# Two expert tiles added from on-chip memory, and gathered rows weighted on TensorE

## The reference

```python
w = jnp.take_along_axis(scores, idx, axis=-1)      # the two chosen experts of each token
w = w / jnp.sum(w, axis=-1, keepdims=True)
combine = jnp.sum(jax.nn.one_hot(idx, N_EXPERTS, dtype=F32) * w[..., None], axis=1)
gate = jnp.einsum('td,edf->tef', t, w_gate_l)
up = jnp.einsum('td,edf->tef', t, w_up_l)
act = jax.nn.silu(gate) * up * combine[..., None].astype(gate.dtype)
return jnp.einsum('tef,efd->td', act, w_down_l).reshape(B, N, D)
```

## Time and profile before

| what | us |
|---|---|
| three runs | 2059.05, 2059.27, 2053.49 (median 2059.05) |
| the profiled execution, its own time | 2056.28 |
| its span, first to last instruction | 2054.5 |
| TensorE busy | 1912.6 (93%) |
| VectorE busy | 1080.4 (53%) |
| ACT busy | 884.8 (43%) |
| GpSimd busy | 314.5 (15%) |
| mean granted TensorE clock | 0.976 of full |

### The profile page before, as it was taken

One profiled execution on the slowest core, in us unless ns is written; L12 is line 12 of the kernel. 1 busy time (PEld: TensorE's weight loads), 2 busy tenths in 40 slices (PEclk: granted clock), 3 DMA queues, 4 the chain that ended last, 5 costly groups with the idle time before them and its releaser, 6 DMA issues. The chain is left out here.

```text
span 2054.5 us, 31276 instructions
## 1 busy us (share of the span) xinstructions
PE 1912.6 (93%) x12731; PEld 1617.7 (79%) x12731; DVE 1080.4 (53%) x1766; ACT 884.8 (43%) x1423; POOL 314.5 (15%) x120
## 2 busy tenths in 40 slices
PE   6999999999999979999779998898999998899993
PEld 4899866699999857777578997677999987577762
DVE  4385367641433256777573734665243334577763
ACT  4443455532222235566454435555222233466653
POOL 1303100032224120000111121000212331000003
PEclk9999999999999999999979999999999999999996
DMA  7422477725612159999441220002222222999954
GB/s 262 131 62 64 147 247 256 240 88 199 211 62 73 47 212 361 315 309 318 156 167 44 75 72 13 1 1 92 89 67 72 73 68 114 376 422 369 311 189 174
DMA packets 163921, 336.34 MB, mean 164 GB/s; under 512 B 10434, under 2 KB 121666, under 8 KB 149316
## 3 DMA queue, kind: packets, MB, share of 16 engines
q1 hardware_dynamic: 151488, 299.63, 41.9%
q0 software_dynamic: 5760, 20.97, 2.7%
q10 hardware_dynamic: 6532, 13.74, 2.1%
HBM read 334.58 MB, written 53.74 MB: 189 GB/s over the span
## 5 line engine op out<-in xcount | busy, mean ns | idle before, releaser
L728 POOL TENSOR_TENSOR wlo<-raw,whi 128x2048 fp32r<-128x2048 f32 x46 | 216.1, 4697 | 1053.2 <-ACT whi L752 1053.2
L2007 DVE TENSOR_TENSOR xw_gu_lo<-xw_gu_raw,xw_gu_hi 128x2048 fp32r<-128x2048 f32 x96 | 218.9, 2284 | 53.7 <-ACT xw_gu_hi L1788 35.6
L171 PE MATMUL psum<-h_hi,whi 128*128 128x320 f32 (+2 forms) x896 | 215.3, 313 | 9.0 <-DVE h_lo L156 6.5
L171 PE MATMUL psum<-h_hi,wlo 128*128 128x320 f32 (+2 forms) x896 | 213.0, 310 | 0.0
L171 PE MATMUL psum<-h_lo,whi 128*128 128x320 f32 (+2 forms) x896 | 213.0, 310 | 0.0
L171 PE MATMUL psum<-whi,h_hi 128*128 128x256 f32 x720 | 210.2, 292 | 0.5 <-ACT v_tok L866 0.5
L171 PE MATMUL psum<-wlo,h_hi 128*128 128x256 f32 x720 | 203.6, 283 | 0.0
L171 PE MATMUL psum<-whi,h_lo 128*128 128x256 f32 x720 | 203.6, 283 | 0.0
L1788 ACT ACTIVATE xw_gu_hi<-xw_gu_raw 128x2048 fp32r<-128x2048 f32 x96 | 178.1, 1907 | 7.6 <-DMA xw_gu_raw<-w_e_up 7.6
L2159 PE MATMUL psum<-xw_d_raw,act_T 128*128 128x512 f32 x400 | 179.9, 592 | 0.9 <-ACT act_T L1818 0.9
L832 ACT ACTIVATE prob<-psum,small_stats 128x640 f32<-128x640 f32 (+1 forms) x160 | 112.0, 705 | 133.1 <-DVE small_stats L1194 133.0
(11 more groups left out here) (319 smaller groups left out, 3657.3 us busy)
## 6 DMA issues: line engine op xcount, KB each, us to landing
xw_d_raw<-w_e_down SPq DMA_DIRECT2D x50, 1024.0 KB, 9.0
xw_gu_raw<-w_e_gate SPq DMA_DIRECT2D x48, 1024.0 KB
xw_gu_raw<-w_e_up SPq DMA_DIRECT2D x48, 1024.0 KB
raw<-w_in SPq DMA_DIRECT2D x46, 1024.0 KB, 5.4
wm_rest<-w_mod SPq DMA_DIRECT2D x40, 1024.0 KB, 5.3
y_rows<-y_sel SPq DMA_DIRECT2D x50, 512.0 KB, 9.5
h_sel<-h_rows SPq DMA_DIRECT2D x48, 512.0 KB, 7.5
h_rows<-c_zero ACTq DMA_DIRECT2D x5, 2560.0 KB, 11.2
```

The source lines that it names most:

```text
L171: mm = pe.matmul(dst, st, mv[q], start=start and n == 0, stop=stop and n == 2)
L728: pool.tensor_tensor(wlo[i % 2][:, :, :], raw[i % 2][:, :, :], whi[i % 2][:, :, :].bitcast(F32), ALU.subtract).then_inc(w_lo, 1)
L2007: dve.tensor_tensor(gu_lo[i % 2][:, n, :, :], gu_raw[i % 2][:, n, :, :], gu_hi[i % 2][:, n, :, :].bitcast(F32), ALU.subtract).then_inc(x_l ...
```

## The change

The results of tiles 23 and 24 are no longer stored and gathered. They stay in the two y_sel buffers, and TensorE adds them by products with a matrix `kept_w` of 128 slots by 128 tokens, one for each of the two tiles and five token tiles, which holds the token's weight where the token sits in that slot and zero elsewhere. A token's row number in the kept tiles is turned into row `row_kept` for the gather; that row of y_rows is cleared once, early in layer 0, by a small DMA on ACT's queue. The gathers wait for the stores of tiles up to 22. The weighting by ACT and VectorE goes: the gathered rows are multiplied on TensorE by diagonal matrices `w_diag` which hold the weights. All 32 products of a token tile accumulate in one PSUM region, already turned. VectorE builds marks and diagonals at the stage's start, TensorE turns the marks, VectorE copies them out of PSUM. The gather buffers lie elsewhere, and the low parts of the next layer's weights stand behind the first residuals.

```diff
--- before.py
+++ after.py
@@ -512,7 +512,13 @@
 
-y_ab = [at(f"y_ab{t}", [P, 2, D], (20 + 8 * t) * K if t < 4 else Z + 104 * K) for t in range(TT)]
+y_ab = [at(f"y_ab{t}", [P, 2, D], off) for t, off in enumerate((28 * K, 40 * K, Z + 104 * K, Z + 80 * K, Z + 88 * K))]
+pos_g = at("rows_gathered", [P, 2, TT], Z + 141 * K + 256, I32)
+w_diag = at("combine_diag", [P, 2, TT, P], RT + 2560)
+kept_w = [at(f"kept_tile_w{h}", [P, TT, P], RT + 8000 * h) for h in range(2)]
+kept_mark = [at(f"kept_tile_marks{h}", [P, TT, P], Z + 32 * K + 2560 * h) for h in range(2)]
+kept_key, kept_f, kept_r, kept_v = (at(f"kept_{x}", [P, 2, n], RT + 10592 + off) for x, n, off in (
+    ("key", TT, 0), ("factor", TT, 64), ("rows", 2 * TT, 128), ("weights", 2 * TT, 224)))
 sq_e = [at(f"sq_e{i}", [P, KD, P], Z + (112 + 4 * i) * K) for i in range(2)]
...
@@ -589,10 +595,14 @@
     return (n if kind == "s" else NE + n) * P
+row_kept = row0(N_TILES - 2)
+assert row0(N_TILES - 1) == row_kept + P and row_kept + 2 * P == SLOTS and (N_TILES - 2) % 2 == 1
 LOGIT_STEPS = 4
 ROUTE_STEPS = 15
 ROW_STEPS = 28
 IDX_STEPS = 44
+GATHER_STEPS = 46
+KEPT_STEPS = 78
 
...
@@ -987,6 +997,8 @@
     branch_high(2)
+if first and n == 2:
+    act.dma_start(y_rows[row_kept:row_kept + 1, :], a["c_zero"][0:1, :]).then_inc(s_rows0, 16)
 if first and 2 <= n < 7:
...
@@ -1739,8 +1751,6 @@
     sp.dma_start(fin_bc[:, :], a["final_norm_g"].partition_broadcast(P)).then_inc(f_g, 16)
-store_y(N_TILES - 2)
-store_y(N_TILES - 1)
 if last:
...
@@ -1762,13 +1772,14 @@
             in_=h_tok[:, t, :], in_offset=None).then_inc(k_s, 16)
-pool.wait_ge(y_st[0], 16 * ((N_TILES + 1) // 2))
-pool.wait_ge(y_st[1], 16 * (N_TILES // 2))
+pool.wait_ge(r_st, GATHER_STEPS)
+pool.wait_ge(y_st[0], 16 * ((N_TILES - 1) // 2))
+pool.wait_ge(y_st[1], 16 * ((N_TILES - 2) // 2))
 for t in range(TT):
     for s in range(2):
         pool.indirect_dma_start(
-            out=y_ab[t][:, s, :], out_offset=None, in_=y_rows,
-            in_offset=bass.IndirectOffsetOnAxis(ap=pos_ab[:, s, t:t + 1], axis=0)).then_inc(y_ld[t], 16)
+            out=y_ab[t][:, s, :], out_offset=None, in_=y_rows[0:row_kept + 1, :],
+            in_offset=bass.IndirectOffsetOnAxis(ap=pos_g[:, s, t:t + 1], axis=0)).then_inc(y_ld[t], 16)
 if last:
...
@@ -1854,16 +1865,8 @@
         act.activation(whi[c][:, :, :], raw[c][:, :, :], ACT.Copy).then_inc(nx_hi, 1)
-def scale_a(t):
-    act.wait_ge(y_ld[t], 32)
-    act.activation(y_ab[t][:, 0, :], y_ab[t][:, 0, :], ACT.Copy, scale=w_ab[:, 0, t:t + 1]).then_inc(m_za, 1)
-
-scale_a(0)
 if not last:
-    scale_a(1)
     for t in range(TT - 1):
-        if t + 2 < TT:
-            scale_a(t + 2)
         if t >= 2:
...
@@ -1998,6 +1999,29 @@
 assert n_st[0] == IDX_STEPS
+rows_2t, w_2t = pos_f[:, 0:2 * TT], w_ab[:, :, :].rearrange("p s t -> p (s t)")
+step(dve.tensor_scalar(kept_r[:, 0, :], rows_2t, float(row_kept), None, ALU.min))
+step(dve.tensor_copy(pos_g[:, :, :].rearrange("p s t -> p (s t)"), kept_r[:, 0, :]))
+assert n_st[0] == GATHER_STEPS
+for h in range(2):
+    step(dve.scalar_tensor_tensor(out=kept_r[:, h, :], in0=rows_2t, scalar=row_kept + P * h - 0.5, in1=rows_2t,
+                                  op0=ALU.is_gt, op1=ALU.mult))
+    step(dve.scalar_tensor_tensor(out=kept_v[:, h, :], in0=rows_2t, scalar=row_kept + P * h - 0.5, in1=w_2t,
+                                  op0=ALU.is_gt, op1=ALU.mult))
+step(dve.tensor_tensor(kept_r[:, 0, :], kept_r[:, 0, :], kept_r[:, 1, :], ALU.subtract))
+step(dve.tensor_tensor(kept_v[:, 0, :], kept_v[:, 0, :], kept_v[:, 1, :], ALU.subtract))
+step(dve.tensor_tensor(kept_key[:, :, :], kept_r[:, :, 0:TT], kept_r[:, :, TT:2 * TT], ALU.add))
+step(dve.tensor_tensor(kept_f[:, :, :], kept_v[:, :, 0:TT], kept_v[:, :, TT:2 * TT], ALU.add))
+for h in range(2):
+    step(dve.tensor_scalar(kept_key[:, h, :], kept_key[:, h, :], -(row_kept + P * h - 1.0), None, ALU.add))
+for h in range(2):
+    for t in range(TT):
+        step(dve.tensor_scalar(kept_mark[h][:, t, :], iota_1[:, :], kept_key[:, h, t:t + 1], kept_f[:, h, t:t + 1],
+                               ALU.is_equal, ALU.mult))
+for s in range(2):
+    for t in range(TT):
+        step(dve.tensor_scalar(w_diag[:, s, t, :], ident[:, :], w_ab[:, s, t:t + 1], None, ALU.mult))
+assert n_st[0] == KEPT_STEPS - 2
 
...
@@ -2034,6 +2058,12 @@
 h_low(1)
+dve.wait_ge(k_t, KD + 1)
+for h in range(2):
+    dve.tensor_copy(kept_w[h][:, 0:4, :].rearrange("p t s -> p (t s)"), psum[:, 7 - 2 * h, :])
+step(dve.tensor_copy(kept_w[0][:, 4, :], psum[:, 6, 0:P]))
+step(dve.tensor_copy(kept_w[1][:, 4, :], psum[:, 6, P:2 * P]))
+assert n_st[0] == KEPT_STEPS
 lo(2, "g")
...
@@ -2049,17 +2079,13 @@
 
-if not last:
+def next_low(c):
     dve.wait_ge(x_gu, N_TILES)
-    for c in range(2):
-        dve.wait_ge(nx_hi, c + 1)
-        dve.tensor_tensor(wlo[c][:, :, :], raw[c][:, :, :], whi[c][:, :, :].bitcast(F32),
-                          ALU.subtract).then_inc(nx_lo, 1)
+    dve.wait_ge(nx_hi, c + 1)
+    dve.tensor_tensor(wlo[c][:, :, :], raw[c][:, :, :], whi[c][:, :, :].bitcast(F32),
+                      ALU.subtract).then_inc(nx_lo, 1)
+
 for t in range(TT + 4):
-    if t < TT:
-        dve.wait_ge(m_za, t + 1)
-        dve.scalar_tensor_tensor(out=y_ab[t][:, 0, :], in0=y_ab[t][:, 1, :], scalar=w_ab[:, 1, t:t + 1],
-                                 in1=y_ab[t][:, 0, :], op0=ALU.mult, op1=ALU.add).then_inc(m_zb, 1)
     if last and 3 <= t < TT + 3:
...
@@ -2071,6 +2097,8 @@
     ins.then_inc(x_step, 1)
+if not last and 1 <= t < 3:
+    next_low(t - 1)
 if last and 2 <= t < TT + 2:
...
@@ -2176,10 +2204,18 @@
 gate_up_first()
+pe.wait_ge(r_st, KEPT_STEPS - 2)
+for h in range(2):
+    for t in range(4):
+        pe.transpose(psum[:, 7 - 2 * h, t * P:(t + 1) * P], kept_mark[h][:, t, :], ident[:, :])
+for h in range(2):
+    mm = pe.transpose(psum[:, 6, h * P:(h + 1) * P], kept_mark[h][:, 4, :], ident[:, :])
+mm.then_inc(k_t, 1)
 turn_h(1)
 turn_act(0)
 gate_up(1)
 turn_h(2)
+pe.wait_ge(r_st, KEPT_STEPS)
 down(0)
...
@@ -2208,11 +2244,17 @@
 for t in range(TT):
-    pe.wait_ge(m_zb, t + 1)
     if t >= 2:
         pe.wait_ge(x_step, t - 1)
-    for f in range(KD):
-        mm = pe.transpose(flat(t % 2)[:, f * P:(f + 1) * P], y_ab[t][:, 0, f * P:(f + 1) * P], ident[:, :])
+    for h in range(2):
+        for f in range(KD):
+            pe.matmul(flat(t % 2)[:, f * P:(f + 1) * P], y_sel[1 - h][:, f * P:(f + 1) * P], kept_w[h][:, t, :],
+                      start=(h == 0 and f % 4 == 0), stop=False)
+    pe.wait_ge(y_ld[t], 32)
+    for s in range(2):
+        for f in range(KD):
+            mm = pe.matmul(flat(t % 2)[:, f * P:(f + 1) * P], y_ab[t][:, s, f * P:(f + 1) * P], w_diag[:, s, t, :],
+                           start=False, stop=(s == 1 and f % 4 == 3))
     mm.then_inc(m_zt, 1)
...
```

More of the change, by code:

```diff
@@ L571, in build @@
             "shift_router_step", "shift_logits_ready", "shift_diag_ready", "shift_row_ready", "shift_row_kept"))
-        k_t, k_a, k_d, k_s, k_pk = (sem(x) for x in ("x_gained_turned", "x_gained_kept", "h_tok_ready", "h_rows_written",
+        k_t, k_a, k_d, k_s, k_pk = (sem(x) for x in ("x_gained_or_kept_marks_turned", "x_gained_kept", "h_tok_ready", "h_rows_written",
                                                      "first_rows_marked"))
@@ L576, in build @@
             "act_T_kept", "down_ready", "y_sel_first_half", "y_sel_second_half"))
-        m_za, m_zb, m_zt = (sem(x) for x in ("y_a_scaled", "y_summed", "y_turned"))
+        m_zt = sem("y_summed_in_turn")
         x_step = sem("moe_residual")
@@ L716, in _ @@
                     if first:
-                        sp.wait_ge(s_rows0, 16 * 5)
+                        sp.wait_ge(s_rows0, 16 * 6)
                 @block.gpsimd
@@ L1873, in _ @@
                     else:
-                        for s in range(TT + 3):
-                            if s + 1 < TT:
-                                scale_a(s + 1)
+                        for s in range(2, TT + 3):
                             if 2 <= s < TT + 2:
```

## The result

The changed kernel runs in 2084.39 us (median of 2081.86, 2082.18, 2086.59 and 2087.78), the kernel before in 2058.94 (four runs): ratio 1.0131, 95% interval 1.0106 to 1.0156. It is slower by 25 us. The forecast was 2075.4, its range 2067 to 2087; one of the four executions lies above that range. The profiled execution took 2081.86, its span is 2080.1, 25.6 more than before.

A forecast was written before the change was run, and what follows sets the result against it. TensorE, busy 93%, was taken as the bound, with holes at both expert stages' ends. 10.2 + 7.5 + 0.2 = 17.9 us gave 2074.2 or 2077.0 by base; forecast between them 2075.4, own range 2070 to 2082, with lost cover 2067 to 2087.

The forecast's parts named there:

- The price of a product: TensorE in the tails: each f32 128x128 product is two instructions and takes 0.222 us, 7.1 us a token tile.
- Gathers: End of each expert stage: gathers wait only for tile 22's store, start near 1007 in layer 0, never waited for.
- Layer 0's tail: End of layer 0's expert stage: TensorE's last product ends at 1056.2 against 1045.97, costing +10.2 us.
- Layer 1's tail: End of layer 1's expert stage: the last square starts at 2051.8 against 2044.34, costing +7.5 us.
- just in time: Layer 1's tail on ACT: a square and a scaling end at 2051.6, before the last square starts at 2051.8.
- The stage's start: Start of both expert stages: new VectorE steps, transposes and copies mostly fit idle time, costing 0.2 us for both layers.
- the cover is gone: Rival at the stage's start: VectorE steps cost twice the row's, about +8 us in all, 2083; chance 0.05.
- the fast case: Rival in TensorE's tails: products cost only a transpose, 0.11 us each, giving 2038; chance 0.05.

The follow-up runs named there:

- e11: The changed kernel again, unchanged, on one chip with the kernel before: 2076.82 us against 2057.01, ratio 1.0085.
- e4: The changed kernel with the two last stores back and the gathers waiting for all 25 stores: 2098.31 us.
- e12: The kernel before, unchanged, profiled a third time, in the same batch as e11: 2055.95 us.
- e6: The changed kernel with gathered rows weighted and summed on ACT and VectorE again, added by 8 identity products, no diagonals: 2061.96 us against 2057.14, ratio 1.0025.
- e7: As e6, but only tile 24 is kept and tile 23 is stored and gathered: 2058.51 us against 2057.14, ratio 1.0011.
- e9: The kernel before with ten unused 128x128 VectorE steps added in tiles 4 to 8: 2058.26 us against 2059.17, ratio 0.9999.
- e10: e7 with some kept products issued early in TensorE's idle time and the next layer's low parts behind the last residual: 2080.42 us against 2059.17, ratio 1.0098.
- e3: The changed kernel without the 16 products per token tile with the two kept tiles, their part of the sum left out: 2053.68 us.
- e8: The changed kernel with its ten diagonals built by two VectorE instructions instead of ten: 2085.02 us against 2059.17, ratio 1.0127.
- e5: The kernel before, unchanged, profiled a second time: 2054.83 us, one execution.

## Why the prediction was right, and which term was not

The direction, the place and the mechanism of the tails held: TensorE fills its idle time and then sets the pace with the new products. That the first measurement, 2084.39, fell inside the range of 2067 to 2087 is in part luck. The forecast's own range ended at 2082; the rest was put there for the lost cover on VectorE, and that did not happen. The sum of the parts was 17.9 us; measured against before in the same batch the change costs 19.8 (e11) and 25.5 in the first result.

*The price of a product.* 0.222 us predicted; 320 instructions of each line at a pitch of 3.57 / 32 = 0.112 us, so 0.223. The groups of the page, over the whole span:

```profile
L2251 PE MATMUL psum<-kept_tile_w,y_sel 128*128 128x128 f32 x320 | 37.5, 275 | 1.7 <-issue 1.7
L2256 PE MATMUL psum<-combine_diag,y_ab 128*128 128x128 f32 x320 | 37.4, 275 | 0.0
```

A transpose of the same shape still takes 0.11. The rule of the Trainium skill ("TensorE: Matmul & The Clock Gate", Terms) that transpose mode is four times faster for FP32 is again not what this case shows; the ratio is two.

*Gathers.* Start near 1007 predicted. 1007.62 in e11, 1010.48 in the changed kernel, where the whole stage lies 3 us later. Never waited for, as predicted; e4 shows what they are worth.

*Layer 0's tail.* From the last copy to the last product 39.2 predicted (1016.98 less 0.02, to 1056.2), 39.7 in both profiles. In e11 the last copy ends at 1016.94, as before, and the prediction can be read off line by line: last product 1056.63 against 1056.2, next layer's first square 1064.07 against 1063.6.

```profile
1016.25 0.69 DVE L2054 COPY y_sel<-psum 128x512 f32<-128x512 f32 x1 [3.70 <-PE psum L2187]
...
1052.89 3.74 PE L2256 MATMUL psum<-combine_diag,y_ab 128*128 128x128 f32 x32
...
1064.07 1.06 ACT L812 ACTIVATE sq_e<-x_T 128x1024 f32<-128x1024 f32 x1 [4.14 <-PEq L133]
```

*Layer 1's tail.* +7.5 predicted, +9.0 measured. From the copy to the last product 38.4 predicted, 38.7 measured (2022.76 to 2061.50). The missing 1.1 us is the step "just in time": the prediction set the end of ACT's scaling (2051.6) against the start of the last square (2051.8), but it is the turning before that square which has to wait for it. The turning needs the region that ACT is still scaling from, and TensorE stands 2.30 us ahead of it.

```profile
2057.76 3.74 PE L2256 MATMUL psum<-combine_diag,y_ab 128*128 128x128 f32 x32
...
2064.67 1.06 PE L2243 MATMUL psum<-ident,x_T 128*128 128x128 f32 x8 [2.30 <-ACT y_tok L1887]
...
2065.77 1.02 ACT L1883 ACTIVATE sq_f<-psum 128x1024 f32<-128x1024 f32 x1 [1.16 <-PE psum L2243]
```

*The stage's start.* This term was mis-sized: 0.2 us for both layers, 7.2 in the profile after. Two parts:

- Without late updates it is 2.2: 0.2 in layer 0 and 2.0 in layer 1. The marks cost 0.40 us each with their gap (4.02 for ten), not 0.315; they take two scalars a partition, the form of the earlier trace rows one. That is 0.9 us over the sum, where no slack was left: in layer 1 the low part of tile 1 starts 23.7 us behind the first pick product, in e12 23.2. And there seven of the first products of tile 1 run 0.43 us apart, where in e12 they are 0.23 apart: 1.4 us. The sum had no term for the clock at a stage's start. The prediction read the turning at 766.39 as TensorE back at full rate; the rows just behind it in the same profile (770.45 and 770.88 above) show the products of tile 1 at about half of it.
- The other 5 us go with late updates: they are the difference between two profiles of the same program. The profile of before does not hold them, and its rows gave no way to foresee them. The prediction's rival "the cover is gone" has the place and the size (+8), but another mechanism: VectorE's steps were not slow, they were hidden as planned (0.24 us idle left ahead of the low part), and it was TensorE that stood, waiting for ACT.

The whole forecast, 2075.4, lies 1.4 us from the changed kernel's 2076.82 without late updates and 9.0 from its 2084.39 with them. Two small sums of the prediction are off by one in the last place: the chances of its cases add up to 0.92 for slower and 0.03 for no change (it has 0.91 and 0.04), and the fast case of layer 0 ends at 1038.2, not 1038.1.

*What the change is worth, part by part* (each against before in its own batch): two kept tiles with early gathers +4.8 (e6); the weighting on TensorE besides, +19.8 (e11), so about 15 for 80 further products (17.9 us by their pitch), and the ten diagonals, that replace scaling and adding on engines which had time; one kept tile +1.4 (e7).

*Open.* Whether late updates belong to a chip or to its condition at the time wasn't told apart: no batch ran twice on the same chip. Whether the kernel before shows them too is seen only in e9, which is that kernel but for ten steps. The first pair of profiles is mixed, after with and before without. What makes TensorE's updates late is not known. Whether e10 beats the kernel before without late updates wasn't run. Of the versions that ran none beats it: e9 is the same kernel in substance, and e3 leaves work out.

## What to carry to other kernels

Before work is moved to the engine with the highest busy share to save a wait, price it in that engine's own instructions: here a hole of 14 us was filled with 36 us of products a layer. Weighting and adding were free on ACT and VectorE, since these waited anyway; on TensorE they are on the path. When a stretch differs that the change didn't touch, profile the unchanged kernel again in the same batch before looking for a cause in the code: e8 and e9 went after diagonals that had nothing to do with it. And before an update is called late, see whether the engine that waits for it started late: in these profiles some updates are only missing from the record.

## What the runs showed of the hardware

- *Late updates behind TensorE.* In six profiles (before, e5, e6, e7, e11, e12) ACT's copy starts 0.03 to 0.04 us behind the last pick product's end, in the eight others 2.8 to 4.9 us behind it. Smaller lags behind TensorE stand in tails (1.12 us in e3, 1.51 and 1.74 in e4, 2.71 in e10), always while indirect transfers of GpSimd run. VectorE's small steps follow each other in 0.04 us in all fourteen. The Trainium skill ("Perfetto Trace Analysis", Tensor Engine Instruction) says that the end shown for a product is an estimate and that its update follows once PSUM has acknowledged the write; that order fits, but in the profiles without late updates all of it takes 0.04 us, and where the microseconds come from stays open.
- *GpSimd beside VectorE.* An indirect gather is issued in 0.94 us alone, and in 2.84 and 1.88 us while a two-input instruction of VectorE runs (e7). The Trainium skill ("SBUF — State Buffer", SBUF: two separate sides) says that a VectorE instruction with both inputs in SBUF and a GpSimd instruction that reads SBUF exclude each other from a shared pair of ports, for the whole instruction. The trace agrees: two low parts run from 1015.57 to 1020.06, and each of the two issues ends 0.8 us behind the end of one of them (1017.85 and 1020.06).
- *The clock after a short stop.* In e11 the granted clock is 1.00 behind 1.11 idle us (the window below; 16 products in 7.13 us). In the changed kernel's profile it was 0.74 and 0.79 with 5.94 idle us, and the same products took 9.06. In the kernel before, after pauses of 2.46, 0.86 and 1.07 us within 6 us, products run 0.43 us apart that elsewhere run 0.23 apart. The clock has two levels, 2.4 and 1.2 GHz; a fraction is the mean over the stretch named.

```profile
756.00:764.20 8.20, 7.16 (x18) 3.29 (x19) 7.03 (x20) 0.99 (x1) 1.94 (x3) 1.00 0.70 271
```
